# Head statistics from the squares' high and low halves in place of one four-byte product

## The reference, cut to what matters

```
h = rmsnorm(x, mix_norm);  z = h @ w_in
q, k, v = z[..., 0:1536], z[..., 1536:3072], z[..., 3072:4608]    # 12 heads x 128 each
q = rope(rmsnorm(q, q_norm), pos)      # the norm runs over the 128 values of each head
k = rope(rmsnorm(k, k_norm), pos)
```

## Time and profile before

| | |
|---|---|
| median of the runs | 2306.87 us (2306.67 to 2307.57) |
| the profiled execution | 2305.88 us, its span 2304.1 us |
| mean granted TensorE clock | 0.998 |
| PE busy | 2272.9 us (99%) |
| DVE, ACT, POOL busy | 1406.2 (61%), 977.4 (42%), 538.9 us (23%) |
| q and k phase with its statistics | about 880 to 1040 us of the span |

### The profile page before, as it was taken

How to read it: one execution, slowest core, us unless ns; L and a number is a source line. 1 busy time by engine, 2 the same in 40 slices (tenths; PEclk the granted TensorE clock), 3 DMA queues, 4 the chain that set the end, 5 groups by cost and what they waited for, 6 DMA issues and landing times.

```text
span 2304.1 us, 47426 instructions
## 1 busy us (share of the span) xinstructions
PE 2272.9 (99%) x18546; PEld 2255.2 (98%) x18546; DVE 1406.2 (61%) x1416; ACT 977.4 (42%) x1203; POOL 538.9 (23%) x565
## 2 busy tenths in 40 slices
PE   7899999999999999999999999999999999999999
PEld 6899999999999999999999999999999999999999
DVE  5575457776455667886757677665555455545555
ACT  5444333343343543444445555444443334433442
POOL 4794016661000113764405540010000000000000
PEclk9999999999999999999999999999999999999999
DMA  8879787777787678758958865568787777757764
GB/s 234 240 227 311 229 248 250 249 248 256 233 244 225 196 233 261 225 180 271 306 156 304 284 199 185 183 192 264 245 245 225 239 246 243 224 183 227 245 201 139
DMA packets 434678, 535.65 MB, mean 232 GB/s; under 512 B 27712, under 2 KB 415800, under 8 KB 430728
## 3 DMA queue, kind: packets, MB, share of 16 engines
q1 hardware_dynamic: 419696, 511.65, 70.4%
q0 software_dynamic: 3216, 11.75, 1.5%
q10 hardware_dynamic: 11664, 10.84, 1.4%
HBM read 510.95 MB, written 109.10 MB: 269 GB/s over the span
## 4 chain that ended last, share of the span: by engine, by line
PE 87%; DVE 5%; POOL 4%; DMA 2%; issue 2%; ACT 1%; SPq 0%; ACTq 0%; DVEq 0%; POOLq 0%
PE pa L1255 28%; PE pa L1257 27%; PE pa L1256 27%; DVE w_lo L887 2%; POOL c_exp L1707 2%; DVE head_sd L1023 1%; POOL pre L1703 1%; DMA raw<-in_ffn_w_gate 1%; ACT w_hi L574 1%; PE pb L1341 1%; PE pb L1512 1%; DMA raw<-in_ffn_w_up 1%; PE pb L1497 1%; DVE up_v L1027 0%; POOL b_tmp L1700 0%
## 5 line engine op out<-in xcount | busy, mean ns | idle before, releaser
L887 DVE TENSOR_TENSOR w_lo<-raw,w_hi 128x1024 fp32r<-128x1024 f32 x736 | 940.1, 1291 | 640.5 <-ACT w_hi L574 635.6
L1255 PE MATMUL pa<-xg_hi,w_hi 128*128 128x264 f32 x3968 | 1136.7, 286 | 9.3 <-DVE w_lo L887 9.2
L1256 PE MATMUL pa<-xg_lo,w_hi 128*128 128x264 f32 x3968 | 1128.6, 284 | 0.0
L1257 PE MATMUL pa<-xg_hi,w_lo 128*128 128x264 f32 x3968 | 1127.2, 284 | 0.0
L574 ACT ACTIVATE w_hi<-raw 128x1024 fp32r<-128x1024 f32 x736 | 767.2, 1055 | 744.5 <-PE pa L1257 701.7
L1255 PEld LDWEIGHTS pa<-xg_hi,w_hi 128*128 128x128 f32 x3968 | 748.2, 189 | 14.1 <-issue 9.9
L1256 PEld LDWEIGHTS pa<-xg_lo,w_hi 128*128 128x128 f32 x3968 | 746.7, 188 | 0.6
L1257 PEld LDWEIGHTS pa<-xg_hi,w_lo 128*128 128x128 f32 x3968 | 746.9, 188 | 0.0
L1256 PE MATMUL pa<-act_lo,w_hi 128*128 128x264 f32 x1632 | 463.9, 284 | 0.0
L1255 PE MATMUL pa<-act_hi,w_hi 128*128 128x264 f32 x1632 | 463.5, 284 | 0.0
L1257 PE MATMUL pa<-act_hi,w_lo 128*128 128x264 f32 x1632 | 463.1, 284 | 0.0
(11 more groups left out here) (307 smaller groups left out, 1637.8 us busy)
## 6 DMA issues: line engine op xcount, KB each, us to landing
raw<-in_ffn_w_gate SPq DMA_DIRECT2D x172, 512.0 KB, 4.9
raw<-in_ffn_w_up SPq DMA_DIRECT2D x172, 512.0 KB, 5.4
out_kv_s<-in_cache_kv_w SPq DMA_DIRECT2D x165, 512.0 KB
raw<-in_ffn_w_down SPq DMA_DIRECT2D x160, 512.0 KB, 4.6
raw<-in_w_in SPq DMA_DIRECT2D x152, 512.0 KB, 4.9
raw<-in_w_out SPq DMA_DIRECT2D x32, 512.0 KB, 4.4
tab<-ssm_tab SPq DMA_DIRECT2D x8, 1664.0 KB, 8.9
raw<-in_w_ssm_branch SPq DMA_DIRECT2D x16, 512.0 KB, 4.3
```

Of the source, the lines that this page charges most:

```text
L887: dve.tensor_tensor(w_lo[:, slot], raw[:, slot], w_hi[:, slot].bitcast(f32), ALU.subtract).then_inc(lo_ready, 1)
L1255: pe.matmul(out, wh, hi, start=first, stop=False)
L1256: pe.matmul(out, wh, lo, start=False, stop=False)
L1257: return pe.matmul(out, wl, hi, start=False, stop=last)
```

## The change

Two f32r tiles are laid over `hid_v` and `sq_v`: `hsq_hi` and `hsq_lo`. ACT writes the squares twice, rounded to float32r into `hsq_hi` and in full into `sq_v`. DVE subtracts, in place over `sq_v`, in pass x at j = 0 behind the low half of that j. PE waits for that subtraction and does two float32r products for each head, accumulated, in place of one product of float32 operands. `head_w` becomes a float32r tile.

```diff
+    head_w = tile("head_w", [P, P], f32r)
+    hsq_hi, hsq_lo = tile("hsq_hi", [P, 2, T], f32r, RT + 24 * T), tile("hsq_lo", [P, 2, T], f32r, RT + 32 * T)
...
                     if x:
                         act.wait_ge(stat_done, x)
+                    act.activation(hsq_hi[:], gate_v[:], ACT.Square)
                     act.activation(sq_v[:], gate_v[:], ACT.Square).then_inc(head_sq, 1)
...
-            dve.memset(head_w[:], 1.0 / HD)
+            dve.memset(head_w[:].bitcast(f32), 1.0 / HD)
...
                         split_lo(ph, i, j + LEAD)
                         if name == "u" and i == 0 and j == 1:
                             root(1)
+                        if j == 0 and 1 <= x <= NH:
+                            dve.wait_ge(head_sq, x)
+                            dve.tensor_tensor(hsq_lo[:], sq_v[:], hsq_hi[:].bitcast(f32), ALU.subtract).then_inc(head_sqlo, 1)
...
-                pe.wait_ge(head_sq, x)
+                pe.wait_ge(head_sqlo, x)
                 pe.wait_ge(*((sd_ready, 2) if x == 1 else (head_sd_ready, x - 1)))
                 for u in range(2):
-                    ins = pe.matmul(pb[:, u, 0:T], head_w[:], sq_v[:, u, :], start=True, stop=True)
+                    pe.matmul(pb[:, u, 0:T], head_w[:], hsq_hi[:, u, :], start=True, stop=False)
+                    ins = pe.matmul(pb[:, u, 0:T], head_w[:], hsq_lo[:, u, :], start=False, stop=True)
                 ins.then_inc(stat_done, 1)
```

More of the change, by code:

```diff
@@ L210, in build_layer @@
     sd = tile("sd", [P, T])
-    ident, mean_w, head_w, ones = (tile(n, [P, P]) for n in ("ident", "mean_w", "head_w", "ones"))
+    ident, mean_w, ones = (tile(n, [P, P]) for n in ("ident", "mean_w", "ones"))
+    head_w = tile("head_w", [P, P], f32r)
     vec = tile("vec", [P, NV])
@@ L320, in build_layer @@
     u_ready, u4_zero, u4_loaded, spilled, const_loaded = sems("u_ready u4_zero u4_loaded spilled const_loaded")
-    head_sq, stat_done, head_sd_ready, head_inv, t1_ready, rot_ready, cos_ready, qk_ready = sems(
-        "head_sq stat_done head_sd_ready head_inv t1_ready rot_ready cos_ready qk_ready")
+    head_sqlo, head_sq, stat_done, head_sd_ready, head_inv, t1_ready, rot_ready, cos_ready, qk_ready = sems(
+        "head_sqlo head_sq stat_done head_sd_ready head_inv t1_ready rot_ready cos_ready qk_ready")
     heads_t, rows_ready, rows_stored, v_new_ready, samples_t, samples_ready, qk_new_ready = sems(
```

## The result

The changed kernel takes 2334.03 us, the median of five runs (2333.25 to 2336.82), against 2306.99 for the kernel before (2306.67 to 2309.13, five runs): a ratio of 1.0118 (95% interval 1.0106 to 1.0129), 27 us slower. 2334.3 was predicted, but two terms of that sum, the pass and the clock, were off in opposite directions, and the experiments show by how much.

The account below looks back on a forecast made before the run. A circle through DVE and ACT, not PE, was taken to set the head phase's pace. Profiled 2305.88 plus 26.3 for the passes and 1.1 for the clock, plus 1.0 from that execution to the median, gave 2334.3 us; range 2320 to 2343.

Parts of the forecast that it names:

- the pass: Head phase, from one `gate_v` to the next: 15.17 us where it was 12.95, 2.22 more, without the clock.
- the clock: PE's longer waits may drop its granted clock to 0.50: 0.1 us a pass allowed, 1.1 in all, at most 6.6.
- What bounds the kernel: Head statistics: a circle through DVE and ACT, 12.95 us a pass, sets the pace, though PE is 99% busy.
- PE's product: PE's head product: four float32r matmuls take 0.48 us in place of 0.93, 0.45 less, gained in pass 1 only.
- ACT's second square: ACT ahead of the next high half: 0.55 us more, so the first low half starts 2.92 behind `gate_v`.
- The subtraction and its hindrance: DVE behind the first low half: subtraction of 0.71 us plus 0.74 of hindrance by POOL, ending 5.50 behind `gate_v`.
- What is queued behind the wait: ACT's root, late behind PE's product, delays the third high half; DVE waits 1.37 us, reciprocal at 9.13, before 6.91.
- The sum: All head-phase passes added: last head product 26.8 us later, less 0.45 for the shorter product, +26.3.
- A gain by a shorter PE product: PE sets the head phase's pace and the rest is hidden: 5.4 us less, 2301.5; chance 0.05.
- Only the added work counts: Head phase: the added work counts, not PE's wait; 0.9 us more a pass, 2317 in all; chance 0.08.
- rival 3: The clock falls in every pass and the head product lies in the slow stretch: 6.6 us more, 2339.8; chance 0.12.
- rival 4: DVE's subtraction blocked longer, up to 1.75 us, or hindrance the full 1.15: 2340 to 2349; chance 0.05.

Follow-up runs that it names:

- Experiment 2: The kernel before, with one float32r head product per head on the squares' high half only, low halves left out: 2306.43 us, ratio 0.9997.
- 8: The kernel before, with ACT's square moved behind the high half of j = 0 of the next pass: 2306.55 us, ratio 0.9991.
- Experiment 1: The kernel before, with only ACT's second square added ahead of the next high half, its result unread: 2309.02 us, ratio 1.0007.
- experiment 4: The changed kernel, with 16 unread float32r products in PE's queue ahead of its wait for the subtraction: 2336.37 us, ratio 1.0120.
- experiment 5: The changed kernel, with ACT's root moved from behind the high half of j = 1 to that of j = 2: 2319.25 us, ratio 1.0057.
- 3: The kernel before, with PE's head product also waiting for the low half of j = 0, no work added: 2321.69 us, ratio 1.0054.

## Why the prediction was right

- **What bounds the kernel.** Right, and the point on which all else hung. Experiment 2 shows that PE's time is worth nothing in this phase, pass 1 left out; 8, that PE sets the pace only once the link from `gate_v` through the square to the high half is cut.
- **PE's product.** Its four matmuls start 0.12 apart, after a first distance of 0.23 (the last product: 1058.56, 1058.79, 1058.91, 1059.03). The saving appears only in pass 1, where `gate_v` came 15.19 behind the first one, not 15.60: 0.41 for 0.45.
- **ACT's second square.** The first low half was to begin 2.92 behind `gate_v`; it was 2.90. Experiment 1 prices it at 0.06 a pass in the q part and 0.2 to 0.3 in the late passes; that a later start meets less hindrance is what the earlier trace rows had shown.
- **The subtraction and its hindrance.** 5.50 was predicted for its end; in experiment 4, where no fall of the clock disturbs the pass, the low half behind it starts at 5.32 (951.43 - 946.11). So the hindrance up to there is about 0.6, not 0.74.
- **What is queued behind the wait.** DVE's new wait was to be 1.37; it is 1.39. Experiments 5 and 3 show the mechanism from both sides, up to the fourteenth `gate_v`: the root's place is worth 12.6 us and takes another 2.0 of the clock's with it, and a wait without work costs 11.8.
- **The pass.** 15.17 was predicted without the clock; experiment 4 has 15.13 to 15.15, and 15.3 to 15.4 in the late passes, for which I had 15.4 and 15.65. What I said would be seen in the changed kernel's own timeline, 15.2 in each pass and PE idle for about 3 us, isn't there as such: its passes are 15.9 and 14.7 in turn, and PE's waits 2.5 to 2.8 and 1.4 to 1.8, since the clock disturbs them.
- **The clock.** The mechanism was right, its size wasn't. I allowed 0.1 a pass, at most 0.6. The fall came in six of eleven passes, not in each, and one with a fall is 1.15 longer than the next: 0.45 of waiting for the fourth high half, where I had bounded the excess at 0.4; 0.26 more because its low half then meets POOL (1.39 from start to start against 1.13), which I hadn't seen; and the rest lies in the next pass, which is shorter than the undisturbed 15.14 by 0.40. There POOL is ahead: the subtraction doesn't meet it and takes 0.69 for 1.24. Net it is 2.0 us by experiment 4, for 1.1. Without its undisturbed passes these parts couldn't be told from each other.
- **The sum.** From the first head product to the last it is 1058.56 - 889.16 = 169.4, against 141.5 before: 27.9, less the 0.45 of the shorter product 27.5; predicted were 26.3 and 1.1, together 27.4. That this fits to a tenth is partly luck: the undisturbed passes 2 to 11 came out 0.6 shorter in all than reckoned (152.1 in experiment 4 for 152.75), the clock 0.9 us dearer. The medians differ by 27.0.
- **The rivals.** A gain by a shorter PE product is excluded by 2. "Only the added work counts" is about what experiment 5 builds: 14.03 a pass, where I had put 13.85. Of the clock that falls in every pass (rival 3): it fell in six, the head product lay in the low stretch only in pass 2, and the cost was 2.0, not 6.6. The subtraction (rival 4) took 0.69 to 0.70 or 1.24, never 1.75.

Open remains what POOL's rotation would cost at another place in its program: that it hinders DVE is read from the traces, and no experiment moved it.

## What to carry to other kernels

An engine that is busy for 99% of a stretch need not set its pace: take one pass, lay the engines' starts side by side, and look for a circle that is longer than the busy engine's own work. Before a product is made cheaper by a step on another engine, ask who waits for it in a queue: here a wait without any work cost 12 us and the second square 1.4, and moving the root and the squares in ACT's program turned 27 us lost into 4.6 gained.

## What the runs showed of the hardware

- The waits of PE ahead of the changed kernel's head product were 2.68, 1.79, 1.58, 2.69, 1.56, 2.69, 1.57, 2.76, 1.37, 2.54 and 1.36 us, in order. Each of the five of 2.5 and more had a granted clock of 0.50 for 3.4 us with it or behind it; of the six of 1.8 and less one had (1.79), and none of 1.7 and less in experiment 5. They alternate because a slow stretch uses up PE's room: 15 matmuls at 0.22 in place of 0.12 put PE back by 1.5, so the next wait is short, and of these short ones only the 1.79 brought a fall. The wait of 2.2 us for `att_lo` is in all twelve profiles; in nine the clock fell with it, in those of experiments 2, 3 and 5 it didn't: at that length it isn't the same from run to run.
- The Trainium skill (SBUF — State Buffer, "Who interferes with whom") says that a VectorE instruction with two inputs in SBUF and a GpSimd instruction that reads SBUF block each other, the second one until the first is done. The rows agree: a low half beside POOL took 1.77 for 1.23, the subtraction 1.24 for 0.70, and the POOL piece that began 0.01 behind a low half took 1.82 for 0.75 (experiment 1), about that low half's length more. What I hadn't expected is how much of a delay this takes back: three low halves that started 0.52 later took 0.47 less.
